# Attention heads in pairs on two halves of TensorE's output partitions, softmax denominators from sums of probability tiles made by GpSimd

## What is computed

```
hl = layer_norm(xl) * (1 + sc_l) + sh_l ;  hc = layer_norm(xc) * (1 + sc_c) + sh_c
z  = h @ w_in                                  # q, k, v of the groups and the gates
A: 6 query heads, 2 key/value heads, head width 64, RMS norm of q and k, rotary positions
B: 4 differential heads = 8 softmax maps of q/k width 32, value width 64
   o = rms_norm(o1 - lam * o2) * (1 - lam_init)
C: 6 latent-attention heads, q/k width 64 + 32 rotary, value width 64
s = q @ k.T * scale ; p = softmax(s) ; o = p @ v
y = concat(o * silu(gate)) @ w_out
x = layer_norm(alpha * x + gt * y)
```

## Time and profile before

| | us |
|---|---|
| median of 3 runs (1125.14 to 1128.49) | 1128.35 |
| the profiled execution | 1133.72 |
| its span in the trace | 1131.9 |
| TensorE busy in the span | 1020.0 |
| attention of layer 0 (first max tile to first transposed gate) | 265.1 to 542.1 |
| attention of layer 1 | 832.0 to 1060.1 |

### The profile page before, as it was taken

The page is one execution under the profiler, slowest core; times in us unless marked ns, Lnnn a source line. Parts: engine busy times, 40 slices in busy tenths (PEclk is TensorE's granted clock), DMA queues, the critical chain, the costliest instruction groups (busy, mean ns, idle before and its releaser), DMA issues.

```text
span 1131.9 us, 12643 instructions
## 1 busy us (share of the span) xinstructions
PE 1020.0 (90%) x4527; PEld 712.2 (63%) x4527; DVE 555.1 (49%) x925; ACT 406.4 (36%) x765; POOL 316.2 (28%) x265
## 2 busy tenths in 40 slices
PE   4799999997999999999798179899979999999893
PEld 2478767985565465656687169789855545565573
DVE  5419131234444557651239856541644455763237
ACT  2522122324445355534310062232344455554320
POOL 2227222442021000001254436343622011010264
PEclk8799999996999999999999589899969999999897
DMA  9756441207312210010631112122263221001321
GB/s 364 255 172 219 165 165 39 75 30 168 85 46 50 54 29 15 16 63 1 223 112 56 56 47 66 56 72 74 66 140 70 56 56 39 21 16 57 149 75 74
DMA packets 46989, 101.63 MB, mean 90 GB/s; under 512 B 10024, under 2 KB 17136, under 8 KB 44880
## 3 DMA queue, kind: packets, MB, share of 16 engines
q1 hardware_dynamic: 45488, 95.58, 28.3%
q10 hardware_dynamic: 1440, 5.24, 1.1%
HBM read 71.33 MB, written 5.26 MB: 68 GB/s over the span
## 4 chain that ended last, share of the span: by engine, by line
PE 74%; DVE 11%; POOL 4%; SPq 3%; ACT 3%; DMA 3%; issue 2%; POOLq 0%; ACTq 0%; DVEq 0%
PE banks L837 16%; PE banks L660 13%; PE banks L661 12%; PE banks L662 12%; PE banks L816 9%; PE banks L793 5%; SPq L492 3%; PE banks L671 2%; DMA area_g<-in_w_ada_dram 2%; DVE stats L1225 1%; DVE area_b L1432 1%; PE banks L834 1%; DVE negmax L1338 1%; PE banks L850 1%; PE banks L724 1%
## 5 line engine op out<-in xcount | busy, mean ns | idle before, releaser
L1338 DVE TENSOR_REDUCE negmax<-banks 128x1 f32<-128x768 f32 (+1 forms) x200 | 169.5, 850 | 185.8 <-PE banks L793 148.4
L660 PE MATMUL banks<-w_split,area_a 128*128 128x512 f32 (+3 forms) x624 | 236.3, 379 | 16.9 <-DVE area_a L1498 10.1
L837 PE MATMUL banks<-area_z,vals 128*65 128x512 f32 x480 | 246.4, 602 | 0.9 <-ACT area_z L1030 0.5
L661 PE MATMUL banks<-w_split,area_a 128*128 128x512 f32 (+3 forms) x624 | 233.2, 374 | 0.0
L662 PE MATMUL banks<-w_split,area_a 128*128 128x512 f32 (+3 forms) x624 | 232.6, 373 | 0.0
L1135 POOL TENSOR_TENSOR w_split<-w_raw,w_split 128x512 fp32r<-128x512 f32 (+4 forms) x124 | 145.8, 1182 | 262.3 <-ACT w_split L936 262.3
L1030 ACT ACTIVATE area_z<-banks 128x512 f32<-128x512 f32 x260 | 150.8, 594 | 146.0 <-PE banks L816 144.3
L936 ACT ACTIVATE w_split<-w_raw 128x512 fp32r<-128x512 f32 (+4 forms) x124 | 70.2, 585 | 285.2 <-PE banks L662 285.1
L816 PE MATMUL banks<-area_a 96*128 96x512 f32 (+6 forms) x532 | 167.3, 411 | 3.9 <-DMA area_a<-m_row 3.6
L660 PEld LDWEIGHTS banks<-w_split,area_a 128*128 128x128 f32 x624 | 119.8, 192 | 49.1 <-issue 16.4
L662 PEld LDWEIGHTS banks<-w_split,area_a 128*128 128x128 f32 x624 | 119.5, 192 | 19.1
(11 more groups left out here) (133 smaller groups left out, 1077.6 us busy)
## 6 DMA issues: line engine op xcount, KB each, us to landing
area_g<-in_w_ada_dram SPq DMA_DIRECT2D x16, 1024.0 KB, 5.2
w_raw<-in_w_in_dram SPq DMA_DIRECT2D x32, 512.0 KB, 3.7
area_a<-parts SPq DMA_DIRECT2D x54, 192.0 KB
area_g<-in_w_ada_dram SPq DMA_DIRECT2D x16, 512.0 KB, 5.1
w_raw<-in_w_out_dram SPq DMA_DIRECT2D x16, 512.0 KB, 4.1
area_a<-parts SPq DMA_DIRECT2D x72, 96.0 KB
area_b<-in_x_dram SPq DMA_DIRECT2D x8, 512.0 KB, 9.6
x_mid<-area_b ACTq DMA_DIRECT2D x6, 512.0 KB, 2.6
```

The source lines that it names most:

```text
L660: nc.tensor.matmul(dst, a[0], b[0], start=first, stop=False)
L661: nc.tensor.matmul(dst, a[0], b[1], start=False, stop=False)
L837: mm = nc.tensor.matmul(banks[0:65, 5, :], vals[:, step, vh, :], pr, start=(step == 0), stop=(step == TILES - 1))
L1338: nc.vector.tensor_reduce(negmax[:, n % 2, t:t + 1], src, AX.X if t < CT else AX.XY, ALU.max, negate=True).then_inc(max_read, 1)
```

## The change

Heads are worked on in pairs p = 0 to 9 (units 2p and 2p + 1). The values lose their column of ones. A mix is one matmul for each head of the pair, the first written to output partitions 0 to 63, the second to 64 to 127 of the same bank. `o_t` then holds both heads on 128 partitions, and one transpose serves both. The denominators come from sums of the probability tiles: GpSimd adds the six latent steps of each head (`sum_probs`, ten additions of 128x512 per pair), VectorE adds the two halves of the context tile in layer 0 (`sum_context`), and TensorE multiplies each 128 columns of the sums by one column of ones (`denominators`: 12 products of one column per pair in layer 0, 8 in layer 1). The score ring has 4 banks, the probability ring 8 tiles, max tiles have banks 4 and 5, mixes bank 6, and bank 7 is shared by context outputs, maxima and denominators. The context maxima of a pair are one max tile. The order on each engine is written out by hand for a pair. Loads are arranged anew (shared keys of group A are loaded once).

```diff
-RING, MAXES, MROWS, OTRS, SPLITS, MLAS = [], [], [], [], [], []
-STEPS = range(-4, NUNIT + 1)
+def max_tiles(L):
+
+    tiles = [(u, t) for u in range(2) for t in GROUPS[1]]
+    return tiles + (["ctx"] if L < DEPTH - 1 else [])
+
...
+EARLY = 6
+RING = []
...
+    for _p in range(NPAIR + 1):
+        now = _p < NPAIR
+        if now:
+            RING += [("s", _L, _p, s, u) for s in range(4) for u in range(2)]
+        if _p:
+            RING += [("o", _L, _p - 1, g) for g in ((1, 0) if _L < DEPTH - 1 else (1,))]
+        if head_pair(_p + 3):
+            RING += [("mla", _L, 2 * _p + 6, part) for part in mla_parts(_L)]
+        if now:
+            RING += [("s", _L, _p, s, u) for s in (4, 5) for u in range(2)]
+        if head_pair(_p + 3):
+            RING += [("mla", _L, 2 * _p + 7, part) for part in mla_parts(_L)]
+        if now and _L < DEPTH - 1:
+            RING += [("s", _L, _p, "ctx", u) for u in range(2)]
...
                         pe.wait_ge(p_ready, N_P[k])
+                    elif k[0] == "o":
+                        pe.wait_ge(o_read, N_O[k])
                     else:
                         pe.wait_ge(ring_free, N_RING_FREE[k])
...
-                    pe.wait_ge(max_read, m - ago)
-                b0 = max_bank(m, u)
-                s, rows = slots[:, n % NSLOT], MAXROWS[family(u)]
-                q = s[0:rows, 0, t * P:(t + 1) * P]
-                if t < CT:
-                    mm = nc.tensor.matmul(banks[:, b0, 0:NCTX], q, s[0:rows, 2, 0:NCTX], start=True, stop=True)
+                if p == 0 and i >= 3:
+                    pe.wait_ge(max_read, m - 3)
+                elif p:
...
+                    for u in range(2):
+                        f = operands(2 * p + u)
+                        for t in range(CT):
+                            mm = nc.tensor.matmul(banks[:, b0 + u, t * NCTX:(t + 1) * NCTX], f[0][0:rows, t * P:(t + 1) * P],
+                                                  f[2][0:rows, 0:NCTX], start=True, stop=True)
                 else:
-                    for i in range(2):
-                        mm = nc.tensor.matmul(banks[:, b0 + i, 0:384], q, s[0:rows, 2, i * 384:(i + 1) * 384],
-                                              start=True, stop=True)
+                    u, t = tile
+                    f = operands(2 * p + u)
...
+            def turn_max(L, p):
...
+                pe.wait_ge(max_read, N_MAX[L, p, len(max_tiles(L)) - 1])
+                if PN[L, p] >= 1:
+                    pe.wait_ge(mrow_ready, PN[L, p])
+                if p > 1 or L:
+                    pe.wait_ge(rec_done, PN[L, p] - 1 if p > 1 else PN[L, 0])
+                nc.tensor.transpose(banks[0:n, 7, 384:512], negmax[:, 0:n], ident[:]).then_inc(mt_filled, 1)
...
+            def mix(L, p, step):
+
+                pe.wait_ge(p_ready, N_P["s", L, p, step, 1])
+                if step == 0 and PN[L, p]:
+                    pe.wait_ge(o_copied, PN[L, p])
...
                 else:
-                    mm = nc.tensor.matmul(banks[0:65, 5, :], vals[:, step, vh, :], pr, start=(step == 0), stop=(step == TILES - 1))
+                    for u in range(2):
+                        mm = nc.tensor.matmul(banks[64 * u:64 * u + 64, 6, :], vals[:, step, value_head(2 * p + u), :],
+                                              prob(L, p, step, u), start=(step == 0), stop=(step == TILES - 1))
                 mm.then_inc(p_used, 1)
...
+            def turn_output(L, p):
+                for g in ((1, 0) if L < DEPTH - 1 else (1,)):
...
+                    for i, t in enumerate(GROUPS[g]):
+                        mm = nc.tensor.transpose(banks[:, r % NP, i * P:(i + 1) * P], o_t[:, t * P:(t + 1) * P], ident[:])
+                    mm.then_inc(ring_filled, 1)
...
+            def denominators(L, p):
                 if L < DEPTH - 1:
...
+                    pe.wait_ge(ctx_copied, N_CTX[L, p])
+                    pe.wait_ge(dve_summed, N_DVE_SUM[L, p, "ctx", 1])
+                pe.wait_ge(mrow_ready, PN[L, min(p + 1, NPAIR - 1)] + 1)
+                pe.wait_ge(pool_summed, N_POOL_SUM[L, p, 5, 1])
+                t0 = q_tiles(L)[0]
+                for t in q_tiles(L):
+                    for u in range(2):
+                        s = ctx_sums[:, p % 2, u, t * P:(t + 1) * P] if t < CT else total(p, u)[:, (t - CT) * P:(t - CT + 1) * P]
+                        at = 256 + 2 * (t - t0) + u
+                        mm = nc.tensor.matmul(banks[:, 7, at:at + 1], s, ones_c[:], start=True, stop=True)
+                mm.then_inc(denom_filled, 1)
...
-                for i in STEPS:
-                    if 14 <= i + 4 < NUNIT:
-                        mla_head(L, i + 4)
-                    steps = score_steps(L)
-                    for j in range(9):
-                        m = j - 2
-                        if 0 <= i + 2 < NUNIT and 0 <= m < len(q_tiles(L)):
-                            max_tile(L, i + 2, q_tiles(L)[m])
-                        if 0 <= i < NUNIT and j < len(steps):
-                            scores(L, i, steps[j])
-                        if 0 <= i < NUNIT and 2 <= j <= len(steps) + 1:
-                            mix(L, i, steps[j - 2])
-                        if j == 3 and 0 <= i + 1 < NUNIT:
-                            turn_max(L, i + 1)
-                        if j == 5 and 0 <= i - 1:
-                            turn_output(L, i - 1)
+                context = L < DEPTH - 1
+                for i in range(len(max_tiles(L))):
+                    max_tile(L, 0, i)
+                turn_max(L, 0)
+
...
+                for p in range(1, NPAIR):
+                    scores(L, p, 0)
+                    max_tile(L, p + 1, 6)
+                    scores(L, p, 1)
+                    max_tile(L, p + 1, 7)
+                    if context:
+                        mix(L, p - 1, "ctx")
+                    else:
+                        mix(L, p - 1, 4)
+                        mix(L, p - 1, 5)
+                    scores(L, p, 2)
+                    max_tile(L, p + 1, 8)
+                    scores(L, p, 3)
+                    turn_output(L, p - 1)
+                    denominators(L, p - 1)
+                    mix(L, p, 0)
+                    turn_max(L, p + 1)
+                    max_tile(L, p + 2, 0)
+                    mix(L, p, 1)
+                    max_tile(L, p + 2, 1)
+                    if head_pair(p + 3):
+                        mla_head(L, 2 * p + 6)
+                    scores(L, p, 4)
+                    max_tile(L, p + 2, 2)
+                    scores(L, p, 5)
+                    max_tile(L, p + 2, 3)
+                    mix(L, p, 2)
+                    max_tile(L, p + 2, 4)
+                    if head_pair(p + 3):
+                        mla_head(L, 2 * p + 7)
+                    mix(L, p, 3)
+                    max_tile(L, p + 2, 5)
+                    if context:
+                        scores(L, p, "ctx")
+                        mix(L, p, 4)
+                        mix(L, p, 5)
+
...
+            def sum_probs(L, p, step):
+
+                for u in range(2):
+                    if step == 1 and PN[L, p] >= 2:
+                        pool.wait_ge(denom_filled, PN[L, p] - 1)
+                    if step > 1:
+                        pool.wait_ge(pool_summed, N_POOL_SUM[L, p, step - 1, u])
+                    pool.wait_ge(p_ready, N_P["s", L, p, step, u])
+                    first = prob(L, p, 0, u) if step == 1 else total(p, u)
+                    nc.gpsimd.tensor_tensor(total(p, u), first, prob(L, p, step, u), ALU.add).then_inc(pool_summed, 1)
...
+                split_block(L, 2)
+                for p in range(NPAIR + 1):
+                    diff = (L, p - 1) in N_NORMED
+                    if p < NPAIR:
+                        sum_probs(L, p, 1)
+                    if p == 0:
+                        split_block(L, 4)
+                    if p < NPAIR:
+                        sum_probs(L, p, 2)
+                    if p and not diff:
+                        gate(L, p - 1)
+                    if p < NPAIR:
+                        sum_probs(L, p, 3)
+                    if diff:
+                        root(("diff", L, p - 1), slice(0, TILES))
+                    if p < NPAIR:
+                        sum_probs(L, p, 4)
+                        sum_probs(L, p, 5)
+                    if p == 0:
+                        split_block(L, 6)
+                    if p == 2:
+                        split_block(L, 10)
+                    if diff:
+                        gate(L, p - 1)
...
+            def output_rows(L, p):
+
...
+                dve.wait_ge(denom_filled, n + 1)
+                nc.vector.reciprocal(rec[:, 0:2 * len(ts)], banks[:, 7, 256:256 + 2 * len(ts)]).then_inc(rec_done, 1)
+                dve.wait_ge(rec_done, n + 1)
+                if n:
+                    dve.wait_ge(gated, n)
...
-                for i in STEPS:
-                    ts = q_tiles(L) if 0 <= i + 2 < NUNIT else []
```

(41 more changed lines are left out.)

644 lines of the change are left out of this document (384 added, 260 removed).

## The result

The changed kernel takes 1206.27 us (median of 4 runs, 1188.87 to 1209.42), the kernel before 1128.11. The ratio is 1.0608, 95% interval 1.0496 to 1.072; it leaves out two executions in a slower state (1209.41 and 1209.42), so it is not the quotient of the two medians. Measured again in six runs, the changed kernel took 1203.75 and the kernel before, in the same call, 1130.18: ratio 1.0648 (1.0618 to 1.0678). The forecast was 1154, range 1115 to 1186. The direction was right; the loss is 74 (1203.75 - 1130.18), not 26.

A forecast was written before the change was run, and what follows sets the result against it. It took the chain max tile, reduction, next max tile (1.67 us a link) as the bound, with matmuls (1.55) pressing too. The terms +2.4 - 0.5 + 12.6 - 1.5 + 7 + 6 = +26 on 1128.35 gave 1154, range 1115 to 1186.

The forecast's parts named there:

- The links: From one max tile through VectorE's reduction to the next: stays 1.67 us, freed matmul time falling into TensorE's waits.
- The price of a pair mix: On TensorE, a latent mix of two heads takes 1.10 us, where two mixes cost 1.72.
- Rival D: The two halves of a pair mix run one after the other, 1.72 us a mix: 1210 us, chance 0.05.
- The denominators: TensorE's one-column products: 0.085 us an instruction, 1.4 us a pair in layer 1 and 2.0 in layer 0.
- The rotations: VectorE's norm and rotations between reductions 5 and 6, pairs 4 to 6: 8.0 us from max tile 5 to 7.
- The clock: TensorE's clock may fall in pair 0 (3.8 us layer 0, 2.4 layer 1) and behind max tile 7's wait (1.7).
- Pairs 0 to 3: First four pairs of each layer: 82.5 us against 80.1 in layer 1, 94.4 against 94.9 in layer 0.
- Pairs 4 to 9 with the end: Later pairs: +12.6 us in layer 1, -1.5 in layer 0; two-head tail adds 2.4 and 3.6.
- Start: Before each layer's first score, four more reductions for both heads' maxima delay it by some 3.5 us: +7.
- GpSimd: Ten additions a pair, 13.2 us, plus gate or power: 15 to 16 of 18.3, hidden with 2 to 3 to spare.
- rival C: GpSimd or what it shares becomes the bound, additions at 1.75 us: +35 on the forecast, 1190 us, chance 0.14.
- Rival B: TensorE's own stream sets the time, so freed time comes through: -39, about 1090 us, if links are 1.4 or less; chance 0.24.

## Why the direction was right and the size wrong

The profiled executions differ by 69.4 (1201.3 - 1131.9), where the sum was 26. So 43 were missing. Term by term:

- **The links** (1.67): right, 1.73, and shown by the halved reduction. That the freed matmul time falls into the waits was right for the links, as the run with one product after the other shows, and 53 arrive in all, mostly outside them. Wrong was the second half of the reading of the kernel before, 0.45 + 0.235 + 0.86 = 1.55 of matmuls in a link: with halved reductions such a link takes 1.25. The 0.86 was read where a context mix follows, and where a max tile follows a mix of one head takes 0.59 (901.89 to 902.48). The 112 of freed matmul time rests on the same 0.86 and was not reached.
- **The price of a pair mix** (1.10): somewhat too high, 0.94 in a run and 1.01 between max tiles. Rival D, one half after the other, is out.
- **The denominators** (0.085 an instruction, 34): mis-sized, 0.11 and 44 by the run without them, 10 of the missing 43. The upper bound, 0.12, was the nearer one.
- **The rotations** (8.0 from max tile 5 to 7): right in layer 1, 8.24.
- **The clock** (3.8 + 2.4 in pair 0 and 1.7 behind a rotation, 11 to 16 in all): this is the step that failed. I let the clock fall only in pair 0 and behind the rotations, for a short time. In the changed kernel's attention it is at half for 136 us, which was 19 before: also before pair 4, in links between which TensorE waits 0.67, and in layer 0 behind the denominators. Behind a rotation it costs 3.2 in the mean, not 1.7, since mixes 4 and 5, the scores, the denominators and mix 0 all stand there: 19 for six rounds instead of 10 (6 x 1.7), so 9 of the missing 43. The 12 long links are another 11, and none of them is in pair 0. Filling TensorE's waits takes 71 us of half clock out of attention (from 150 in the repeated measurement of the changed kernel to 79, by the mean clock from the first turned maxima to the first gate of both layers; 26 in the kernel before) and gives 15 to 19, after paying for the extra matmuls. What the 79 that are left cost was not isolated; since work at half clock takes twice its time, it is at most half of them, some 40.
- **Pairs 0 to 3** (+2.4 in layer 1 and -0.5 in layer 0): +10.1 and +7.0. The price of the denominators explains 0.4 x 3 and 0.7 x 3. The rows of maxima behind SyncE's copies (0 to 1.5, estimated without a row) were mis-sized as a piece of work, 18.1 of issues, but cost nothing measurable as the kernel stands, and 11 in the one with less in its way. The rest goes with the clock, which for these pairs is argued from the windows and the long links, not shown by a run.
- **Pairs 4 to 9 with the end** (+15.0 in layer 1 and +2.1 in layer 0): +26.8 and +18.5, by rounds of 33.1, 34.0 and 32.5 in layer 1 for 29.5, 30 and 30, and of 34.7, 37.6 and 37.9 in layer 0 for 32. Of this the stretches behind the rotations and the denominators (0.4 to 0.7 a round) are shown above.
- **Start** (+7): measured 1.2. The four reductions more did not show, since the max tiles of the kernel before stood waiting for theirs: from the first max tile to the turned maxima it is 7.7 in layer 1 in both kernels (831.95 to 839.68, 863.23 to 870.98). Between the layers there are 5.2 more, not forecast: the transposes of the gates and what follows start at half clock (48 transposes 8.20 instead of 5.49).
- **GpSimd**: hidden, as forecast; rival C is out. The carried 0.7 for a held-up rotation is seen in one instruction of three (L1589, 976 ns for 684). The Trainium skill, "SBUF — State Buffer", section Who interferes with whom, says that a VectorE instruction with two SBUF inputs contends with a GpSimd one that reads SBUF. By that rule it is the instruction that met GpSimd's gate product; the trace agrees (L1589 took 1.12 where L1360 had begun 0.65 before it).

Denominators 10, the stretches behind the rotations 9, the long links 11 and the time between the layers 5, less 6 at the start, are 29 of the 43. The other 14 stay open.

Rival B said 1090, and the kernel with half of each reduction, without denominators and rotations and with the copies moved takes 1093.87. That the numbers meet is luck: B's sum still held 34 for the denominators and all of the rotations. Its mechanism, freed time that comes through once the chain is short, is what those runs show; its point of decision, a link of 1.4 or less, was not reached in the changed kernel.

## What to carry to other kernels

Before halving an engine's work, look for a chain through a second engine that already sets its pace: here max tile, reduction, max tile, 1.67, beside 1.25 of matmuls. The engine's share of busy time, 90%, hid it. The halved part then turns into short waits, and on TensorE waits can also cost clock for what stands behind them. So price not only the wait but also the stretch behind it, at full and at half clock; here the difference was 0 to 5.1 a round. Count a product of one column by its instructions, 0.22 for the two of a float32 block here, and not by its one column.

## What the runs showed of the hardware

- Adding 114 to 178 matmuls to TensorE's waits made the kernel 15 to 19 us faster. One stretch behind such a wait took 8.31 instead of 12.48, at a granted clock of 1.00 instead of 0.50 at its start.
- The granted clock also fell behind a block of one-column products, with TensorE busy all the time: 24 of them in layer 0 (339.08 to 341.75) are followed by a clock of 0.50 and a pair mix of 1.90 (341.75 to 343.65). With the block left out, the clock was 1.00 from 284 to 368, with it 0.92. The round at 318.7 took 24.9, and 20.6 without the block, 4.3 less for 2.67 of products. A block of 16 in layer 1 (929.13 to 930.91) was not followed by the half clock.
- Products of two heads to output partitions 0 to 63 and 64 to 127 of one bank start within 0.007 of each other (930.909 and 930.915).
- A one-column product of a 128x128 float32 block is two instructions of 0.11 each; with a bfloat16 block it is one of 0.04.
- SyncE takes 0.62 to issue one copy inside SBUF, and 28 of them hold its queue for 18.1.
